# One decoder step: even layer's inputs reordered, its norm as a diagonal in the turns, phases on VectorE, the first expert gather turned

## What is computed

```python
even layer:  x += [ sliding-window GQA with sinks (A) || S5 diagonal state space model (B) ](rmsnorm(x))
odd layer:   x += [ RG-LRU (C) || dilated attention (D), three groups with caches of 128, 512, 1024 rows ](rmsnorm(x))
after each:  x += hierarchical MoE(rmsnorm(x)): best of 4 groups, best 2 of its 4 experts, 16 gated MLPs with FF = 256
outputs:     rmsnorm(x) of prompt and samples, and every cache and state moved on by the new tokens
```

## Time and profile before

| | |
|---|---|
| median of 3 runs | 619.79 us (619.42 to 621.38) |
| the profiled execution | 623.26 us |
| its span, first to last instruction | 621.2 us |
| mean granted TensorE clock | 0.979 |
| TensorE busy | 582.7 us, 94% |
| VectorE, ScalarE, GpSimd busy | 247.7, 154.8, 100.3 us |
| DMA | 208.89 MB, mean 336 GB/s |

### The profile page before, as it was taken

One profiled execution on the slowest core, in us unless ns is written; L12 is line 12 of the kernel. 1 busy time (PEld: TensorE's weight loads), 2 busy tenths in 40 slices (PEclk: granted clock), 3 DMA queues, 4 the chain that ended last, 5 costly groups with the idle time before them and its releaser, 6 DMA issues. The chain is left out here.

```text
span 621.2 us, 8411 instructions
## 1 busy us (share of the span) xinstructions
PE 582.7 (94%) x3372; PEld 324.6 (52%) x3372; DVE 247.7 (40%) x594; ACT 154.8 (25%) x329; POOL 100.3 (16%) x131
## 2 busy tenths in 40 slices
PE   5899999899979999999999999999999999999993
PEld 2577877445533434335777556667645543443330
DVE  5993974112842112127621614250113861121116
ACT  5132185121401101025134203163003311010122
POOL 7999710000021110000100001000000021110000
PEclk9899998999979999999999999999989999999997
DMA  9951899999999999999996999999699569999962
GB/s 316 383 68 16 197 390 327 317 425 424 396 398 370 412 420 424 384 318 382 389 412 233 378 371 327 317 357 401 241 425 405 222 232 415 423 420 423 417 191 87
DMA packets 39768, 208.89 MB, mean 336 GB/s; under 512 B 12659, under 2 KB 14387, under 8 KB 23760
## 3 DMA queue, kind: packets, MB, share of 16 engines
q1 hardware_dynamic: 29488, 165.20, 68.8%
q0 software_dynamic: 8640, 39.25, 17.9%
q10 hardware_dynamic: 1600, 3.88, 1.6%
HBM read 198.73 MB, written 43.74 MB: 390 GB/s over the span
## 5 line engine op out<-in xcount | busy, mean ns | idle before, releaser
L2057 PE MATMUL bank<-arena,ring 128*128 128x320 f32 x320 | 88.9, 434 | 0.5 <-PEq L1163 0.5
L1332 PE MATMUL bank<-arena 128*64 128x512 f32 x272 | 77.7, 593 | 0.0
L2057 PEld LDWEIGHTS bank<-arena,ring 128*128 128x128 f32 x320 | 60.1, 190 | 27.3 <-issue 2.5
L1332 PE MATMUL bank<-ring,arena 128*64 128x512 f32 x240 | 70.6, 593 | 0.0
L1251 PE MATMUL bank<-ring,arena 128*128 128x512 f32 x112 | 50.6, 610 | 4.0 <-PEq L1999 2.0
L1736 DVE TENSOR_TENSOR arena<-arena,bank 128x256 f32<-128x256 f32 x16 | 6.7, 421 | 103.7 <-ACT arena L1521 103.7
L1360 PE MATMUL bank<-arena 128*64 128x512 f32 x136 | 41.5, 620 | 5.5 <-issue 3.8
L543 PE MATMUL bank<-xnT,ring 128*128 128x320 f32 x144 | 41.2, 448 | 2.5 <-DVE xnT L872 2.5
L1332 PEld LDWEIGHTS bank<-arena 128*64 128x64 f32 x272 | 25.8, 137 | 33.0 <-issue 32.8
L1332 PEld LDWEIGHTS bank<-ring,arena 128*64 128x64 f32 x240 | 23.6, 137 | 32.9 <-issue 32.8
L1360 PE MATMUL bank<-ring,arena 128*64 128x512 f32 x120 | 36.4, 597 | 4.4 <-issue 3.7
(11 more groups left out here) (440 smaller groups left out, 856.6 us busy)
## 6 DMA issues: line engine op xcount, KB each, us to landing
arena<-in_w_moe SPq DMA_DIRECT2D x51, 1024.0 KB, 21.6
ring<-in_w_moe SPq DMA_DIRECT2D x45, 1024.0 KB, 16.6
out_o_d_old<-in_cache_d_g POOLq DMA_DIRECT2D x2, 7680.0 KB, 40.2
arena<-in_stream_b SPq DMA_DIRECT2D x4, 2560.0 KB, 13.4
out_o_d_old<-in_cache_d_g POOLq DMA_DIRECT2D x1, 8448.0 KB, 29.6
arena<-in_stream_a SPq DMA_DIRECT2D x4, 2048.0 KB, 9.1
ring<-in_w_out_even SPq DMA_DIRECT2D x2, 2048.0 KB, 10.3
ring<-in_w_qkv SPq DMA_DIRECT2D x1, 3072.0 KB, 18.6
```

The costliest lines, as they stand in the source:

```text
L1332: last = nc.tensor.matmul(c.bank[2 + j % 2][half, :], xgT[:, j % 2, q, half], w[i][:, q, :], start=(q == 0), stop=(q == KC - 1))
L2057: last = nc.tensor.matmul(bank(name)[:, 0:TOK], w[:, k, i * P:(i + 1) * P], xnT[:, k, :], start=(k == 0), stop=(k == KC - 1))
```

## The change

It touches three places.

1. **Even mixer, start.** SP asks for the first 48 columns of even_in, then x, small, w_u, and only then for the rest of even_in (semaphore ld_bc, awaited by VectorE before b and c are used). ScalarE squares tile 0 before the sine and takes the root of each tile before the next square. VectorE no longer scales the rows: it makes `rdiag`, the identity times 1/rms, and TensorE's turns are f32 matmuls of the residual with rdiag. VectorE's order is scale 0, scale 1, gain 0, scale 2, gain 1, gain 2. GpSimd grows ph for n = 1, 2 only; VectorE grows it for 4, 8, 16 after cp; rho is filled by ScalarE.
2. **Copy of cache 1**, in three parts: rows 0 to 288 (4.7 MB) on SP's queue behind w_glu, rows 288 to 480 and 480 to 504 (3.1 and 0.4 MB) on GpSimd's queue in the MoE of layer 1, after its second logits.
3. **Router.** `gather_first` has the operands changed over and gives the rows turned: eight matmuls of 128 columns a tile. ScalarE's copies and `turn_first` are gone. S is replaced by L, one one-hot matrix for six combinations of choice and tile, and R by H, made by GpSimd from hs and constants; 12 matmuls of 16 columns give index and scatter index as sums, one VectorE instruction adds an offset. S of the last four experts is made in `last_gates`. The first half of the up product waits for the first half of the turned rows only.

```diff
@@ even mixer, SP
-            sp.dma_start(ev["in"], x["even_in"]).then_inc(ld_in, 16)
+            sp.dma_start(ev["in"][:, 0:3 * PAIRS], x["even_in"][:, 0:3 * PAIRS]).then_inc(ld_in, 16)
...
             c.load_item(sp, IT_U)
+            sp.dma_start(ev["in"][:, 3 * PAIRS:EVEN_COLS], x["even_in"][:, 3 * PAIRS:EVEN_COLS]).then_inc(ld_bc, 16)
             c.load_item(sp, IT_QKV)
...
             c.load_item(sp, IT_GLU)
+            copy_rows(sp, x, 1, 0, SHORT_SPLIT, c.first_copy)
             sp.wait_ge(u_out, 64)
@@ even mixer, GpSimd
-            for n in (1, 2, 4, 8, 16):
+            for n in (1, 2):
                 grow(ph, n, 0)
-            g.tensor_copy(rho[:, 0], r8.unsqueeze(2).broadcast_to([P, PAIRS, PCH]))
...
+            pool.wait_ge(p_own, link.n)
+            g.memset(ev["f1"], 0.0).then_inc(ph_ok, 1)
...
-            for n in (1, 0):
-                copy_d_cache(pool, x, n, copies)
+            copy_d_cache(pool, x, 0, copies)
@@ even mixer, TensorE
-                        last = nc.tensor.transpose(bank(f"x{t}{'ab'[h]}")[:, k * rows:(k + 1) * rows],
-                                                   xn[0:rows, t, (4 * h + k) * P:(4 * h + k + 1) * P], c.ident[0:rows, 0:rows])
+                        last = nc.tensor.matmul(bank(f"x{t}{'ab'[h]}")[:, k * rows:(k + 1) * rows],
+                                                c.resid[0:rows, t, (4 * h + k) * P:(4 * h + k + 1) * P], rdiag[0:rows, t, 0:rows],
+                                                start=True, stop=True)
@@ even mixer, ScalarE
             square(0)
+            act.wait_ge(arg_ok, 2)
+            nc.scalar.activation(sn, ca, ACT.Sin)
+            nc.scalar.activation(cs, cb, ACT.Sin).then_inc(trig_ok, 1)
+            root(0)
             square(1)
-            root(0)
+            root(1)
             square(2)
-            root(1)
             root(2)
+            nc.scalar.copy(rho[:, 0], r8.unsqueeze(2).broadcast_to([P, PAIRS, PCH]))
...
@@ even mixer, VectorE
-                v.tensor_scalar(xn[0:ROWS[t], t], c.resid[0:ROWS[t], t], c.stat[0:ROWS[t], 6 + t:7 + t], None,
-                                ALU.mult).then_inc(xn_ok, 1)
+                v.tensor_scalar(rdiag[:, t], c.ident[:, :], c.stat[:, 6 + t:7 + t], None, ALU.mult).then_inc(xn_ok, 1)
...
+            dve.wait_ge(ld_bc, 16)
...
+            dve.wait_ge(ph_ok, 1)
+            for n in (4, 8, 16):
+                top = [ph[:, r, :, n - 1:n].broadcast_to([P, PAIRS, n]) for r in range(2)]
+                cmul(ph[:, 0, :, n:2 * n], ph[:, 1, :, n:2 * n], ph[:, 0, :, 0:n], ph[:, 1, :, 0:n], top[0], top[1],
+                     ev["pt"][0][:, :, 0:n], ev["pt"][1][:, :, 0:n])
@@ MoE, GpSimd
+            if layer == 1:
+                pool.wait_ge(lg_pe, 2)
+                copy_rows(pool, x, 1, SHORT_SPLIT, SHORT_END, copies)
+                copy_rows(pool, x, 1, SHORT_END, CACHE[1] - NS, copies)
             pool.wait_ge(xg_zero, 1)
+            pool.wait_ge(hs_ok, 1)
+            for d in range(2):
+                for w in range(2):
+                    last = nc.gpsimd.tensor_tensor(m["H"][:, d, :, w, :], m["hs"], m["code"][:, d, w].unsqueeze(2).broadcast_to([P, 6, PAIR_N]),
+                                                   ALU.mult)
+            last.then_inc(H_ok, 1)
             pool.wait_ge(rows_out, 48)
@@ MoE, TensorE
-                        last = nc.tensor.matmul(c.bank[2 + h][:, :], m["Sf"][0:ROWS[t], t].rearrange("p e s -> p (e s)"),
-                                                xn[0:ROWS[t], t, h * 512:(h + 1) * 512], start=(t == 0), stop=(t == 2))
+                        for q in range(4 * h, 4 * h + 4):
+                            last = nc.tensor.matmul(c.bank[2 + h][:, (q % 4) * P:(q % 4 + 1) * P], xn[0:ROWS[t], t, q * P:(q + 1) * P],
+                                                    m["Sf"][0:ROWS[t], t].rearrange("p e s -> p (e s)"),
+                                                    start=(t == 0 and q == 4 * h), stop=(t == 2 and q == 4 * h + 3))
...
-                pe.wait_ge(xt_ok, 2 * j + 2)
+                pe.wait_ge(xt_ok, 2 * j + 1)
                 for q in range(KC):
                     if q == KC // 2:
                         last.then_inc(up_mid, 1)
+                        pe.wait_ge(xt_ok, 2 * j + 2)
...
             gather_first((2,))
-            turn_first()
-            c.keep_clock_up(c.bank[6], 1, 256)
-            pe.wait_ge(S_ok, 3)
...
+            c.keep_clock_up(c.bank[6], 2, 256)
+            pe.wait_ge(H_ok, 1)
+            pe.wait_ge(S_ok, 1)
+            for n in range(6):
+                for d in range(2):
+                    last = nc.tensor.matmul(c.bank[5][:, 0:2 * PAIR_N], m["L"][:, n, :], m["H"][:, d, n].rearrange("p w j -> p (w j)"),
+                                            start=(n == 0 and d == 0), stop=(n == 5 and d == 1))
             last.then_inc(idx_pe, 1)
             c.keep_clock_up(c.bank[6], 1, 256)
@@ MoE, ScalarE
-            nc.scalar.copy(m["rows0"][:, 0:512], c.bank[2][:, :]).then_inc(rows0_a, 1)
...
@@ MoE, VectorE
+            v.tensor_tensor(m["hs"].rearrange("p c j -> p (c j)"), sel6[:, :, 0], sel6[:, :, 1], ALU.add).then_inc(hs_ok, 1)
+            link(v.tensor_reduce(m["odd"], m["sel"].rearrange("p q t (j i) -> p (q t) i j", i=2)[:, :, 1], AX.X, ALU.add))
             place(2, 3)
-            for t in range(3):
-                v.tensor_tensor(m["S"][:, t], iota[:, 1:CAP + 1].unsqueeze(1).broadcast_to([P, E_N, CAP]),
-                                m["tmp"][:, t].unsqueeze(2).broadcast_to([P, E_N, CAP]), ALU.is_equal).then_inc(S_ok, 1)
...
+            link(v.tensor_reduce(pk, m["spos"], AX.X, ALU.add))
+            v.tensor_scalar(m["far"], pk, float(CAP), float(SKIP), ALU.is_ge, ALU.mult)
+            link(v.scalar_tensor_tensor(m["lo"], m["odd"], float(CAP), pk, ALU.mult, ALU.add))
+            link(v.tensor_tensor(m["lo"], m["lo"], m["far"], ALU.add))
+            v.tensor_tensor(m["L"], iota.unsqueeze(1).broadcast_to([P, 6, P]), m["lo"].unsqueeze(2).broadcast_to([P, 6, P]),
+                            ALU.is_equal).then_inc(S_ok, 1)
...
+            v.tensor_scalar(m["idx"].bitcast(U32), c.bank[5][:, 0:2 * PAIR_N].rearrange("p (w j) -> p w j", w=2), float(SKIP), None, ALU.add)\
+                .then_inc(idx_ok, 1)
@@ MoE, VectorE, last_gates
+                for t in range(3):
+                    ins = v.tensor_tensor(m["S"][:, t], iota[:, 1:CAP + 1].unsqueeze(1).broadcast_to([P, 4, CAP]),
+                                          m["tmp"][:, t, E_N - 4:E_N].unsqueeze(2).broadcast_to([P, 4, CAP]), ALU.is_equal)
```

More of the change, by code:

```diff
@@ L351, in copy_cache, with copy_rows @@
     eng.dma_start(dst[:, n * row:(w - NS) * row], old[:, (NS + n) * row:w * row]).then_inc(copies, 16)
+SHORT_SPLIT, SHORT_END = 288, 480
+def copy_rows(eng, x, g, lo, hi, copies):
+    row, dst = 2 * D_H * HD, x[f"o_d{g}_old"]
+    old = x[f"cache_d_g{g}"][0].rearrange("b w t h d -> b (w t h d)")
+    to, at = dst[:, lo * row:hi * row], old[:, (NS + lo) * row:(NS + hi) * row]
+    if (hi - lo) % 48 == 0:
+        to, at = [ap.rearrange("b (a f) -> a b f", f=3 * row) for ap in (to, at)]
+    eng.dma_start(to, at).then_inc(copies, 16)
 def copy_d_cache(eng, x, n, copies):
@@ L362, in copy_long_cache @@
 def copy_long_cache(eng, x, part, copies):
[L365 to L372 removed]
+    n = (CACHE[2] - NS) // 48 * 48
+    if part == 0:
+        copy_rows(eng, x, 2, 0, LONG_SPLIT, copies)
+    else:
+        copy_rows(eng, x, 2, LONG_SPLIT, n, copies)
+        copy_rows(eng, x, 2, n, CACHE[2] - NS, copies)
 def even_mixer_block(c, x, ev, copies, zeroed):
@@ L829, in _, with mean, scale, gain @@
             v, link = nc.vector, Link(dve, d_own)
+            def mean(t):
+                dve.wait_ge(sq_ok, t + 1)
+                link(v.tensor_scalar(c.stat[:, 3 + t:4 + t], c.stat[:, t:t + 1], 1.0 / D, EPS, ALU.mult, ALU.add))
+                v.reciprocal(c.stat[:, 3 + t:4 + t], c.stat[:, 3 + t:4 + t]).then_inc(ms_ok, 1)
+            def scale(t):
+                dve.wait_ge(rs_ok, t + 1)
+                v.tensor_scalar(rdiag[:, t], c.ident[:, :], c.stat[:, 6 + t:7 + t], None, ALU.mult).then_inc(xn_ok, 1)
+            def gain(t):
+                rows = ROWS[t]
+                for h in range(2):
+                    name = f"x{t}{'ab'[h]}"
+                    filled(dve, name)
+                    v.tensor_tensor(c.xnT[:, 4 * h:4 * h + 4, t * P:t * P + rows],
+                                    bank(name)[:, 0:4 * rows].rearrange("p (k r) -> p k r", k=4),
+                                    c.gains[:, 0, 4 * h:4 * h + 4].unsqueeze(2).broadcast_to([P, 4, rows]), ALU.mult)\
+                        .then_inc(d_empty, 1)
             dve.wait_ge(dt_ok, 1)
@@ L1052, in route_consts @@
         k[:, 3 * P + t] = t * P + np.arange(P)
-    k[:, 3 * P + 4:] = np.arange(E_N)[None, :] // 4
+    k[:, 3 * P + 4:3 * P + 4 + E_N] = np.arange(E_N)[None, :] // 4
+    token = np.arange(3)[None, :] * P + np.arange(P)[:, None]
```

(11 more changed lines are left out.)

119 lines of the change are left out of this document (35 added, 84 removed).

## The result

| | before | after |
|---|---|---|
| median of 4 runs each | 619.98 us (619.42 to 621.38) | 612.44 us (611.52 to 614.12) |
| ratio | | 0.9878, 95% interval 0.9849 to 0.9907 |
| the profiled execution, its span | 623.26, 621.2 us | 611.52, 609.6 us |
| mean granted TensorE clock | 0.979 | 0.988 |
| TensorE busy | 582.7 us | 578.6 us |

Faster by 7.5 us, 1.2%. The forecast said 609.4, range 605.5 to 615.5. Between the two profiles lie 11.7 us, so the first question is where those went, the second why the medians show only 7.5.

The account below looks back on a forecast made before the run. TensorE, busy nearly throughout, bounds the kernel; bytes pay only where it waits for them. Start -3.1, both routers -1.6, layer 0's first pair -5.3 and layer 1 -0.4 sum to -10.4 us: 609.4 us, range 605.5 to 615.5.

Parts of the forecast that it names:

- Start, -3.1: Even mixer's start: projection 1.7 us earlier, full clock another 1.7, 0.3 lost at wt's turns; net -3.1 us.
- The first copy, 0: 4.7 MB of cache 1 ahead of U's loads fill a DMA hole; U lands in time, cost 0, bounds 0 and 3.
- Router, -0.8 per layer: Both routers: first gather to first expert product takes 2.05 us instead of 2.82, so -0.8 us per layer.
- First pair of layer 0, -5.3: Layer 0's first expert pair: gather leaves 2.1 us earlier, rows arrive before needed; -5.3 us, bounds -5.5 and -1.4.
- With 5 us, as in layer 1, it is there at 174.9: Layer 0's gather: leaving at 169.9 and taking 5 us, it arrives before the pair needs it at 176.2.
- Taking 8.3 MB out of 75 to 115 us buys nothing by itself: Cache 1's copy leaving its old place gains nothing there, since TensorE shows no wait for weights in that stretch.
- Layer 1, -0.4: End of layer 1: of the last down product's 0.99 us wait for weights, 0.4 us is gained.
- The late gather: Rival: layer 0's gather still comes 1.8 us late behind experts 4 and 5, clock falls; 612.7 us, chance 0.24.
- The late copy in layer 1: Rival: the copy is still in POOL's queue when layer 1's gathers are asked for; +5.5, 614.9 us, chance 0.12.
- The slower one: Rival: the first copy holds up U's loads, TensorE stands 14 us, then half clock; 625.4 us, chance 0.05.
- The turns at the price of four transpositions: Rival, even mixer's start: each f32 turn costs 0.54 us, turns end at 22.2; +5.9, 615.3 us, chance 0.02.
- Nothing moves: Rival, whole kernel: TensorE's work is unchanged and waits saved in one place return at the next; 619.8 us, chance 0.03.

Follow-up runs that it names:

- no copy moved: Changed kernel with the copy of cache 1 back in its old place (start and router changed): 614.03 us, ratio 0.9909 to the kernel before.
- The experiment with 7.9 MB: Changed kernel with 7.9 MB of the cache 1 copy ahead of the loads of U, in place of 4.7: 622.59 us, ratio 1.0063 to the kernel before.
- after again: The changed kernel measured and profiled again, nothing altered: 612.2 us, ratio 0.9886 to the kernel before.
- router only: Kernel before with only the router changed (turned first gather, L and H), start and copies as before: 617.46 us, ratio 0.9974.
- one wait more: Kernel before, but in layer 0 SP's queue asks for weights of experts 6 and 7 only after the first gathered rows land: 618.82 us, ratio 0.9974.
- copy only: Kernel before with only the copy of cache 1 moved (4.7 MB to SP's queue, 3.5 MB to GpSimd's in layer 1's router): 618.73 us, ratio 0.9998.

## Why the prediction was right, point by point

**Start, -3.1.** Right in its parts. Projection 16.49 (16.8 said), wt's turns 34.24 (34.5), GpSimd's phases at 51.08 and VectorE's at 56.6 (51.6 and 57.7), clock full, as the sum had it, though not for the reason given: no copy moved had the same 0.5 us of idle time and the half clock. The working stopped at wt's turns: the half clock near 96 to 104 us was not in it, although before has it too (100 to 104). It cost 3.4 us in the profile of after (6.8 us at half speed) and 1.7 in that of before, so 1.8 of the lead arrive at the MoE. In the other profile of the changed kernel it cost 1.7, and 3.5 arrive. -3.1 lies between the two; the bounds lacked this term.

**The first copy, 0.** Right. It ran at some 340 GB/s from 34 to 40 us, the loads of U were asked for 2.3 us later than before and were there in time. The experiment with 7.9 MB shows how near the edge is: 3.1 MB more cost 10.4 us. The Trainium skill, DMA: Bandwidth & Descriptors, Queues, rings and completion order, has descriptors consumed in ring order on each engine. The trace agrees as far as it goes: U's loads, whose eight issues took 13.52 us from 43.98 on (4.04 in the changed kernel), did not pass the copy, and TensorE waited 8.20 us. Whether order in the ring or a common share of full engines held them, it does not tell.

**Router, -0.8 per layer.** Right: the lead grew by 0.8 between the first product of the MoE and the first expert in layer 0 and between expert 5's request and the first expert in layer 1. The gap is 1.8 us and not 2.05, but the turned gather costs 0.2 more than the old one (3.84 and 2.05 us in place of 3.70 and 1.98).

**First pair of layer 0, -5.3.** The size is right for the profiled execution (5.5), the cause and the scope are not. The step that failed as a cause is "With 5 us, as in layer 1, it is there at 174.9", read as a matter of when the gather leaves. Router alone sent it 2.7 us earlier and it took 8.1 us; copy alone sent it no earlier and it took 4.9. With it falls "Taking 8.3 MB out of 75 to 115 us buys nothing by itself": those bytes had kept the engines full up to the request for experts 4 and 5, and without them they idle from 150 to 154. The third part of the change, costed at nothing, goes with the early gather in every profile that has it, and no time of the changed kernel lies 4 us above the rest; how the idle engines do it is the argument above and not shown.

The scope is where the median missed by 3 us. I took the wait of one execution for that of all and carried the 3.5 us between the profile and the median over unchanged; the profile of after lies 0.9 below its median. But before has executions that by their times lack the wait, 32 of 73. The term counts in the other 41 only. At 5.5 by the profiles it is 5.5 x 41 / 73 = 3.1 in the mean, at 4.2 by the distance of the groups 2.4. With that the sum is -3.1 - 1.6 - 2.4 to 3.1 = -7.1 to -7.8. The mean of the 73 is 619.4, that of the ten 612.6, so 6.9 were measured; the medians of the two comparisons differ by 7.5 and 8.0. Whether this also explains the first comparison is not shown: none of its four executions of before lies in the lower group, and two lie between the groups. So that the forecast of 609.4 came within 3 us, inside its range, is in part luck: the wrong cause and the scope of this term stood beside a range wide enough for both. For the profile the forecast said 612.9; it took 611.52, and the 1.4 between them are less than the 1.7 of the half clock after the barrier at 452 us, which comes and goes: it is in 10 of the 14 profiles, the second one of the changed kernel among them.

**Layer 1, -0.4.** Nothing that holds. The 0.99 us at the last down product is in neither other profile of before, so it comes and goes; after has 0.31 there and after again none. The copy costs there what the pair shows, 0.3.

**The rivals.** The late gather (0.24) happened in five of the seven profiles without the copy's move and in none with it; in no copy moved it cost 1.55, in router only 3.2. The late copy in layer 1 (0.12) is real, 3.6 us in the pair when the copy moves alone, and in the whole change 0.39 to 0.49 us of wait are left of it. There the gather leaves 0.97 us after the first expert product in place of 2.02; that this is what saves it is argued, since no run has the copy and the router without the start. The slower one has its mechanism, at 7.9 MB and not at 4.7. The turns at the price of four transpositions: no, 24 products in 5.95 us, 0.25 each, 1.8 times the 0.136 of a transposition. Nothing moves: no.

## What to carry to other kernels

A late transfer has two causes to tell apart, when it is asked for and what the engines still have to do, and only a run that changes one of them tells which. Look at what the DMA engines do before the loads that stand ahead of it, even 15 us earlier and where no engine waits for a byte: a copy moved out of there was worth nothing by the waits, and the gather was early in all seven profiles that had the engines idle there. A wait in one profile is one sample. Before it becomes a term, look at whether the times of the kernel fall into groups, and profile it again. And two parts of a change can be worth something only together: the copy's move alone, by its profile, lost in layer 1 a good part of what it gained in layer 0, and in the whole change that loss is gone but for 0.4 us.

## What was not expected of the hardware

- The same gather, issued at the same place of the same program, took 5.3, 7.9 and 8.1 us in three executions, and the kernel's times fell into two groups 4.2 us apart by their medians.
- With no other weights asked for, the rows still took 7.0 us beside the last bytes of 6.3 MB of weights that had been asked for 13 to 16 us before the gather.
- After a wait of 8.2 us TensorE ran at half clock for more than 9 us although its profile shows no hole there, and for some 6 after the 3.13 of before. The length of the wait does not settle it: after 1.98 (one wait more) the half clock lasted 6 us, after 2.00 (copy only) 3.4, and of two waits of 1.7 one was followed by it (router only) and one was not (no copy moved).
- Beside GpSimd's fill a tensor_scalar of 128x16 on VectorE took 2.92 us (0.99 in the kernel before). It began 1.9 us earlier and ended at 6.04 as before, just behind the fill's end at 5.89, so the earlier head of even_in brought VectorE nothing.
